# Five matrix products instead of six for each weight tile of the MLPs: high and low operand side by side in three PSUM banks

## The chip, the cores and the metric

One NeuronCore of one Trainium2 chip runs the whole program. TensorE (PE in the profile) multiplies, VectorE (DVE), ScalarE (ACT) and GpSimd (POOL) do the elementwise work, SyncE (SP) and others issue transfers. The metric is device time in microseconds (us) of one launch; lower is better.

## The reference

One inference step of two decoder layers, for a prompt of 512 tokens and 8 sample tokens, 520 columns together. What matters here is that each layer ends with the same MLP over d_model 1024 and d_ff 4096:

```python
def sq_relu_mlp(h, w_up, w_down):
    return jnp.square(jax.nn.relu(h @ w_up)) @ w_down
...
        yp = yp + rmsnorm(mp, g[1])
        ys = ys + rmsnorm(ms, g[1])
        yp = yp + rmsnorm(sq_relu_mlp(rmsnorm(yp, g[2]), w_up[layer], w_down[layer]), g[3])
        ys = ys + rmsnorm(sq_relu_mlp(rmsnorm(ys, g[2]), w_up[layer], w_down[layer]), g[3])
```

Ahead of it stand, in layer 0, attention with a paged cache and gated linear attention, and in layer 1 a recurrent block. The change touches neither.

## The kernel before

Activations lie transposed: features on the 128 partitions, the 520 columns (T) along the free side, in 8 tiles of 128 features (KT). Every product is made from two parts of each operand. A float32 value is split into a high part (type fp32r, read by TensorE at one column a step) and a low part, the rest. The product is high weight by high data, plus high weight by low data, plus low weight by high data.

Weights come in chunks of 256 output features and all 1024 inputs, 1 MB each, by SyncE's queue into RAW (two slots). ScalarE makes the high part W_hi (`split_hi`, L810), VectorE the low part W_lo (`split_lo`, L1285). A chunk has two output tiles of 128 features. For a tile, `step` (L1881) issues for each of 8 input tiles k six products of 260 columns, three pairs over the two halves of the 520 columns. They accumulate in two PSUM banks; tiles alternate between two such pairs of banks (`ch.par`), so that one is emptied while the other is filled.

An MLP is 32 chunks in 4 groups. In a group, chunks 0 to 3 are w_up: VectorE takes the relu out of PSUM, multiplies by the norm's factor and writes it to SBUF (`evicted`, L1683), ScalarE squares it (L1124), VectorE makes U_hi and U_lo of it (`raised`, L1688 and L1690). Chunks 4 to 7 are w_down: their products read U, and VectorE adds each finished tile into ACC (L1717). The first two chunks of each MLP are made by `opening`, which interleaves three tiles with the norm of the stage before.

After the last chunk of an MLP comes the norm of its output: ScalarE squares the 8 tiles of ACC (`square`, L835), TensorE sums the squares with a matrix of ones (`sum_squares`, L1865), ScalarE takes the root (L842), VectorE the inverse (L1306), TensorE spreads it over the partitions (`spread`, L1873), and VectorE scales and adds (L1310, L1316). In layer 0 ScalarE and VectorE also split half a chunk of the next stage between the sixth and the seventh square (`early_hi`, L816, and `early_lo`, L1290). In layer 1 ScalarE also writes ACCG, a scaled copy of ACC (L1237), behind each square.

Each engine's queue is an order written out by hand and runs strictly in that order. Engines wait on semaphores: `tiles_done` counts finished tiles, `banks_free` the emptied banks, `w_lo_ready` the split chunks, `sq_ready` the squares. Names that one memory region shares are aliases: RL is SQ, LL (after) is TMP.

Of the kernel before, what the change touches and what calls it, by code (L numbers as in the profile page):

```python
# [113 lines left out]
def trunk(nc, ctx, a, o):  # L114
# [29 lines left out]
    H_hi = sb("H_hi", [P, KT, T], F32R, r_h)  # L144
    H_lo = sb("H_lo", [P, KT, T], F32R, r_h + KT * TB)
# [615 lines left out]
    def _(act):  # L761
# [332 lines left out]
        def before_odd():  # L1094
# [24 lines left out]
        def mlp(layer, c0):  # L1119
            def raised(ch, i, u, count):  # L1120
                act.wait_ge(banks_free[ch.par[i]], ch.banks_free[i] + 1)
                if u >= 2:
                    act.wait_ge(u_lo_ready, count - 1)
                A(UF[:, i], RL[:, i], ACT.Square).then_inc(uf_ready, 1)  # L1124

            for g in range(4):
                for j in range(8):
                    c = c0 + 8 * g + j
                    if c > c0 and c + 1 < N_CHUNKS:
                        split_hi(Chunk(c + 1))  # L1130
                    if layer == 0 and g == 1 and j == 5:
                        before_odd()
                    if j < 4:
                        for i in range(2):
                            u = 2 * j + i
                            raised(Chunk(c), i, u, 32 * layer + 8 * g + u)
# [110 lines left out]
    def _(ve):  # L1247
# [429 lines left out]
        def mlp(layer, c0):  # L1677
# [622 lines left out]
```

## Time and profile before

| | us |
|---|---|
| median of 3 runs | 1545.1 (1544.49 to 1548.04) |
| the profiled execution, its own time | 1543.63 |
| its span, first to last instruction | 1541.8 |
| PE busy | 1406.3 (91%) |
| DVE busy | 882.3 (57%) |
| ACT busy | 516.7 (34%) |
| mean granted TensorE clock | 0.930 of full |

The span is what the trace's rows add up to; the profiled execution's own time is 1.8 us longer, and the median of the unprofiled runs 1.5 us longer again. Busy time of PE counts overlapping products once and says nothing of how near the engine is to its peak. How far apart two products start is read from how long a row of x of them lasts: start of the last minus start of the first is the row's length less one product's duration.

### The profile page before, as it was taken

The page shows a single profiled execution, that of the slowest core. Times are in us where ns is not written, and L with a number is a line of the kernel's source. Part 1 is how long each engine was busy: PE and PEld are TensorE (multiplying, and loading weights), DVE is VectorE, ACT ScalarE, POOL GpSimd, SP SyncE. Part 2 cuts the span into 40 slices and gives each one's busy share as a digit, 9 for nine tenths or more (in the row PEclk, how much of TensorE's full clock was granted, in tenths as well). Part 3 has the DMA queues.
Part 4 walks back from the last instruction along what each step waited for, and adds up shares of the span by engine and source line. Part 5 has one row for each costly group of instructions (what it writes and reads, how often), then busy time and mean ns, then how long its engine had stood idle before and what let it go on. Part 6 is the DMA issues. An engine that isn't in the chain of part 4 may idle for free.

```text
span 1541.8 us, 26106 instructions
## 1 busy us (share of the span) xinstructions
PE 1406.3 (91%) x11324; PEld 1266.3 (82%) x11324; DVE 882.3 (57%) x1156; ACT 516.7 (34%) x839; POOL 328.7 (21%) x264
## 2 busy tenths in 40 slices
PE   4999957788778698999999999899989999999997
PEld 3999933345334398999999999899989999999997
DVE  3398978766988526624435343689556344353443
ACT  3323254433423424312212122469443122131233
POOL 1085768865777100000000000000000000000000
PEclk8999979877676799999999999999999999999999
DMA  9477699988989831232322322222212323223211
GB/s 320 137 264 232 236 327 382 369 324 326 346 322 346 300 109 55 86 106 83 97 97 82 99 94 83 83 83 83 85 55 88 105 83 101 92 83 103 90 55 56
DMA packets 126856, 249.32 MB, mean 162 GB/s; under 512 B 5251, under 2 KB 107415, under 8 KB 110096
## 3 DMA queue, kind: packets, MB, share of 16 engines
q0 software_dynamic: 18432, 134.23, 22.9%
q1 hardware_dynamic: 103616, 107.13, 21.5%
q10 hardware_dynamic: 4696, 6.32, 1.3%
q8 instruction: 89, 1.46, 0.4%
q14 instruction: 23, 0.19, 0.0%
HBM read 239.99 MB, written 7.73 MB: 161 GB/s over the span
## 4 chain that ended last, share of the span: by engine, by line
PE 58%; issue 25%; DVE 7%; POOL 4%; DMA 3%; ACT 3%; ACTq 0%; POOLq 0%; DVEq 0%
PE PS L1881 46%; PE PS L2074 2%; POOL PROD L680 2%; DMA KV<-in_cache_v,CIDX 2%; DVE SC L1352 1%; PE PS L2216 1%; POOL KV L747 1%; DVE ST L1584 1%; PE PS L2061 1%; PE PS L2158 1%; DMA XSIN<-in_x_sample 1%; PE PS L1865 1%; PE PS L2179 1%; PE PS L2116 1%; PE PS L1975 1%
## 5 line engine op out<-in xcount | busy, mean ns | idle before, releaser
L1881 PE MATMUL PS<-H_hi,W_hi 128*128 128x260 f32 x1936 | 397.7, 287 | 16.7 <-DVE H_lo L1327 9.7
L1881 PE MATMUL PS<-H_hi,W_lo 128*128 128x260 f32 x1936 | 393.4, 285 | 0.0
L1881 PE MATMUL PS<-H_lo,W_hi 128*128 128x260 f32 x1936 | 393.0, 285 | 0.0
L1881 PEld LDWEIGHTS PS<-H_hi,W_hi 128*128 128x128 f32 x1936 | 303.2, 191 | 22.3 <-issue 17.7
L1881 PEld LDWEIGHTS PS<-H_hi,W_lo 128*128 128x128 f32 x1936 | 301.9, 191 | 0.0
L1881 PEld LDWEIGHTS PS<-H_lo,W_hi 128*128 128x128 f32 x1936 | 301.7, 191 | 0.0
L1285 DVE TENSOR_TENSOR W_lo<-RAW,W_hi 128x2048 fp32r<-128x2048 f32 x90 | 208.2, 2313 | 125.9 <-ACT W_hi L810 125.8
L810 ACT ACTIVATE W_hi<-RAW 128x2048 fp32r<-128x2048 f32 x90 | 171.8, 1909 | 266.1 <-PE PS L1881 265.5
L1881 PE MATMUL PS<-U_hi,W_lo 128*128 128x260 f32 x1024 | 206.4, 283 | 0.0
L1881 PE MATMUL PS<-U_lo,W_hi 128*128 128x260 f32 x1024 | 206.0, 283 | 0.0
L1881 PE MATMUL PS<-U_hi,W_hi 128*128 128x260 f32 x1024 | 206.0, 282 | 0.0
L680 POOL TENSOR_TENSOR PROD<-KV,QB 128x1024 f32<-128x1024 f32 x64 | 152.0, 2375 | 120.4 <-DVE SC L1352 91.5
L1717 DVE TENSOR_TENSOR ACC<-ACC,PS 128x520 f32<-128x520 f32 x64 | 44.6, 697 | 201.4 <-PE PS L1881 201.4
L1881 PEld LDWEIGHTS PS<-U_hi,W_hi 128*128 128x128 f32 x1024 | 157.9, 189 | 0.0
L1881 PEld LDWEIGHTS PS<-U_hi,W_lo 128*128 128x128 f32 x1024 | 157.9, 188 | 0.0
L1881 PEld LDWEIGHTS PS<-U_lo,W_hi 128*128 128x128 f32 x1024 | 157.4, 188 | 0.0
L753 POOL MEMSET ACC<- 128x4160 f32 x2 | 7.1, 3572 | 637.3 <-DVE TMP L1310 637.3
L1124 ACT ACTIVATE UF<-SQ 128x520 f32<-128x520 f32 x64 | 40.8, 639 | 253.2 <-DVE SQ L1683 253.2
L2074 PE MATMUL PS<-KV,PM 128*32 128x512 f32 x512 | 88.2, 777 | 23.4 <-DMA KV<-in_cache_v,CIDX 13.6
L1683 DVE SCALAR_TENSOR_TENSOR SQ<-PS,RS 128x520 f32<-128x520 f32 x64 | 44.6, 700 | 109.2 <-PE PS L1881 109.2
L1364 DVE TENSOR_TENSOR PROD<-KV,PS 128x1024 f32<-128x1024 f32 x64 | 77.5, 1210 | 9.0 <-ACT QB L866 8.9
L747 POOL DMA_INDIRECT KV<-in_cache_k,CIDX x64 | 70.4, 1100 | 53.8 <-DVE TMP L1310 23.1
(304 smaller groups left out, 1433.8 us busy)
## 6 DMA issues: line engine op xcount, KB each, us to landing
RAW<-in_w_up SPq DMA_DIRECT2D x32, 1024.0 KB
RAW<-in_w_down SPq DMA_DIRECT2D x32, 1024.0 KB
RAW<-in_w_in_even SPq DMA_DIRECT2D x13, 1024.0 KB
RAW<-in_w_in_odd SPq DMA_DIRECT2D x8, 1024.0 KB
RAW<-in_w_out_even SPq DMA_DIRECT2D x4, 1024.0 KB
RAW<-in_w_out_odd SPq DMA_DIRECT2D x4, 1024.0 KB
x_saved<-X ACTq DMA_DIRECT2D x1, 2080.0 KB, 9.3
X<-x_saved SPq DMA_DIRECT2D x1, 2080.0 KB, 7.8
```

The lines of the kernel that those rows point to most:

```text
L680: nc.gpsimd.tensor_tensor(PROD[:, 1], KV[i % RING][:, 2:4, :], QB[:, None, b % 2, :].to_broadcast([P, 2, 512]), ALU.mult).then_inc(prod1_r ...
L747: po.indirect_dma_start(KV[i % RING].rearrange("p n f -> p (n f)"), None, cache[kind], bass.IndirectOffsetOnAxis(ap=CIDX[:, n:n + 1], axis ...
L810: A(W_hi[:, ch.slot], RAW[:, ch.slot], ACT.Copy).then_inc(w_hi_ready, 1)
L1124: A(UF[:, i], RL[:, i], ACT.Square).then_inc(uf_ready, 1)
L1285: V.tensor_tensor(W_lo[:, ch.slot], RAW[:, ch.slot], W_hi[:, ch.slot].bitcast(F32), ALU.subtract).then_inc(w_lo_ready, 1)
L1352: V.tensor_reduce(k_scores(n, 1), PROD[:, 1].rearrange("p n (j d) -> p n j d", d=DH), AX.X, ALU.add).then_inc(prod1_used, 1)
L1364: V.tensor_tensor(PROD[:, 0], KV[i % RING][:, 0:2, :], PS[:, None, 6 + b % 2, :].to_broadcast([P, 2, 512]), ALU.mult).then_inc(k_used, 1)
L1584: V.scalar_tensor_tensor(ST[:, hp, state(tb, n + 1)], ST[:, hp, state(tb, n)], DECC[:, hp, 8 * tb + n:8 * tb + n + 1], update(n, slice(0, ...
L1683: V.scalar_tensor_tensor(pair(RL[:, i]), tile_banks(ch, i), 0.0, pair(RS[:, 1]), ALU.max, ALU.mult).then_inc(banks_free[ch.par[i]], 1)
L1717: V.tensor_tensor(pair(ACC[:, m]), pair(ACC[:, m]), banks(ch.par[i]), ALU.add).then_inc(banks_free[ch.par[i]], 1)
L1881: t = MM_(PS[:, 2 * bank + j, 0:HALF], w[:, ch.slot, k, cols], x[:, k, half], start=k == 0 and n == 0, stop=k == KT - 1 and n == 2)
L2074: t = MM_(PS[32 * pos:32 * pos + 32, 4, :], PM[:, part % 2, at:at + 32], KV[i % RING][:, pos, :], start=n % 32 == 0, stop=n % 32 == 31)
```

## The change

Chunks 2 to 31 of each MLP (the two of `opening` stay as they were) get another way of multiplying. The high and the low data lie side by side in one tensor of 1040 columns (H for H_hi and H_lo, U for U_hi and U_lo). `joint_step` sends high weight over all 1040 columns in three products (284, 284 and 472 columns) and low weight over the 520 high columns in two (284 and 236). Results of the high data stand in one bank's end and the next one's beginning, and the results of the low data behind them, through a third bank. The columns streamed stay 1560 for each k.

The two parts are added outside TensorE. ScalarE copies the part of the low data to LL (two copies, 48 and 472 columns, `low_copied`). For w_up VectorE adds the PSUM part and LL into RL and then takes relu and factor in place, in a second pass (`joint_evicted`); for w_down it adds first LL and then the PSUM part to ACC (`accumulated`). The last tile of `opening` goes to the two banks of SPREAD (`FOURTH`) and waits for their copy instead of for the first eviction. Some semaphores of other places are merged.

```diff
-    H_hi = sb("H_hi", [P, KT, T], F32R, r_h)
-    H_lo = sb("H_lo", [P, KT, T], F32R, r_h + KT * TB)
+    H = sb("H", [P, KT, 2 * T], F32R, r_h)
+    H_hi, H_lo = H[:, :, 0:T], H[:, :, T:2 * T]
...
+    CUT = 284
...
-            def raised(ch, i, u, count):
-                act.wait_ge(banks_free[ch.par[i]], ch.banks_free[i] + 1)
+            def low_copied(ch, i, q):
+                act.wait_ge(tiles_done, ch.done[i])
+                act.wait_ge(banks_free[ch.par[i]], ch.banks_free[i])
+                first, rest = joint_lo(ch.par[i])
+                A(LL[:, q % 2, 0:LO_CUT], first, ACT.Copy)
+                A(LL[:, q % 2, LO_CUT:T], rest, ACT.Copy).then_inc(ll_ready, 1)
+
+            def raised(i, u, count):
...
+                    for i in range(2):
+                        u, q = 2 * j + i, joint_tile(layer, g, j, i)
+                        if g == 0 and j < 2:
+                            act.wait_ge(banks_free[ch.par[i]], ch.banks_free[i] + 1)
+                        else:
+                            low_copied(ch, i, q)
+                            if j < 4:
+                                act.wait_ge(rl_ready, 28 * layer + 8 * g + u - 3)
+                        if j < 4:
+                            raised(i, u, 32 * layer + 8 * g + u)
...
+            def joint_evicted(ch, i, u, q, count):
+                ve.wait_ge(tiles_done, ch.done[i])
+                ve.wait_ge(ll_ready, q + 1)
+                V.tensor_tensor(RL[:, i], joint_hi(ch.par[i]), LL[:, q % 2], ALU.add).then_inc(banks_free[ch.par[i]], 1)
+                ve.wait_ge(banks_free[ch.par[i]], ch.banks_free[i] + 1)
+                V.scalar_tensor_tensor(RL[:, i], RL[:, i], 0.0, RS[:, 1], ALU.max, ALU.mult).then_inc(rl_ready, 1)
+
+            def accumulated(ch, i, m, q):
+                ve.wait_ge(ll_ready, q + 1)
+                link(V.tensor_tensor(ACC[:, m], ACC[:, m], LL[:, q % 2], ALU.add))
+                ve.wait_ge(tiles_done, ch.done[i])
+                V.tensor_tensor(ACC[:, m], ACC[:, m], joint_hi(ch.par[i]), ALU.add).then_inc(banks_free[ch.par[i]], 1)
...
-                            ve.wait_ge(tiles_done, ch.done[i])
-                            V.tensor_tensor(pair(ACC[:, m]), pair(ACC[:, m]), banks(ch.par[i]), ALU.add).then_inc(banks_free[ch.par[i]], 1)
+                            accumulated(ch, i, m, q)
...
+        def joint_step(ch, i, k, both):
+
+            cols, bank = slice(P * i, P * i + P), 3 * ch.par[i]
+            hi, lo = W_hi[:, ch.slot, k, cols], W_lo[:, ch.slot, k, cols]
+            first, last = k == 0, k == KT - 1
+            MM_(PS[:, bank, 512 - CUT:512], hi, both[:, k, 0:CUT], start=first, stop=False)
+            MM_(PS[:, bank + 1, 0:CUT], hi, both[:, k, CUT:2 * CUT], start=first, stop=False)
+            MM_(PS[:, bank + 2, 0:2 * T - 2 * CUT], hi, both[:, k, 2 * CUT:2 * T], start=first, stop=last)
+            MM_(PS[:, bank, 512 - CUT:512], lo, both[:, k, 0:CUT], start=False, stop=last)
+            t = MM_(PS[:, bank + 1, 0:T - CUT], lo, both[:, k, CUT:T], start=False, stop=last)
+            if last:
+                t.then_inc(tiles_done, 1)
...
-            pe.wait_ge(banks_free[b.par[1]], b.banks_free[1])
+            if c0 == C_IN1:
+                pe.wait_ge(banks_free[b.par[1]], b.banks_free[1])
+            else:
+                pe.wait_ge(rs_copied, opened + 1)
```

The order of instructions on TensorE for one k of a w_down tile, first before and then after (W_hi and W_lo are the weight parts, U the data):

```order
L1881 MATMUL PS<-U_hi,W_hi 128x260 x2
L1881 MATMUL PS<-U_lo,W_hi 128x260 x2
L1881 MATMUL PS<-U_hi,W_lo 128x260 x2
```

```order
L1938 MATMUL PS<-U,W_hi 128x284
L1939 MATMUL PS<-U,W_hi 128x284
L1940 MATMUL PS<-U,W_hi 128x472
L1941 MATMUL PS<-U,W_lo 128x284
L1942 MATMUL PS<-U,W_lo 128x236
```

Six products of 260 columns have become three with the high weight and two with the low weight.

The order on ScalarE at the end of layer 0's MLP, from its last weight split on. Before (L810 splits a chunk, L835 squares a tile of ACC, L816 is `early_hi`):

```order
L810 ACTIVATE W_hi<-RAW 128x2048 x4
L835 ACTIVATE SQ_START<-ACC 128x520 x6
L816 ACTIVATE W_hi<-RAW 128x8x128
L835 ACTIVATE SQ_START<-ACC 128x520 x2
L842 ACTIVATE RS<-PS,EPSC 128x130
```

After (L832, L857 and L838 are the same three; L1146 and L1147 copy the low part of a tile):

```order
L832 ACTIVATE W_hi<-RAW 128x2048
L1146 ACTIVATE TMP<-PS 128x48
L1147 ACTIVATE TMP<-PS 128x472
L1146 ACTIVATE TMP<-PS 128x48
L1147 ACTIVATE TMP<-PS 128x472
L857 ACTIVATE SQ_START<-ACC 128x520 x6
L838 ACTIVATE W_hi<-RAW 128x8x128
L857 ACTIVATE SQ_START<-ACC 128x520 x2
L864 ACTIVATE RS<-PS,EPSC 128x130
```

The squares stood behind the last split alone; now the copies of the last two tiles stand between, and each waits for its tile's products.

The order on VectorE at the same place, before (L1717 adds a tile into ACC, L1290 is `early_lo`, L1306 is the inverse of the norm) and after (L1729 and L1731 add the two parts, L1324 is `early_lo`, L1340 the inverse):

```order
L1285 TENSOR_TENSOR W_lo<-RAW,W_hi 128x2048 [waits w_hi_ready]
L1717 TENSOR_TENSOR ACC<-ACC,PS 128x520 [waits tiles_done]
L1290 TENSOR_TENSOR W_lo<-RAW,W_hi 128x8x128 [waits w_early]
L1717 TENSOR_TENSOR ACC<-ACC,PS 128x520 [waits tiles_done]
L1306 RECIPROCAL RS<-RS 128x130 [waits root_ready]
```

```order
L1319 TENSOR_TENSOR W_lo<-RAW,W_hi 128x2048 [waits w_hi_ready]
L1729 TENSOR_TENSOR ACC<-ACC,TMP 128x520 [waits ll_ready]
L1731 TENSOR_TENSOR ACC<-ACC,PS 128x520 [waits tiles_done,dve_step]
L1324 TENSOR_TENSOR W_lo<-RAW,W_hi 128x8x128 [waits w_early]
L1729 TENSOR_TENSOR ACC<-ACC,TMP 128x520 [waits ll_ready]
L1731 TENSOR_TENSOR ACC<-ACC,PS 128x520 [waits tiles_done,dve_step]
L1340 RECIPROCAL RS<-RS 128x130 [waits root_ready]
```

`early_lo` stood and stands ahead of the last tile's addition, which is now two instructions.

## Rows read from the trace of the kernel before

**Rows 1.** The page: the chain that ended last, by line.

```profile
PE PS L1881 46%; PE PS L2074 2%; POOL PROD L680 2%; DMA KV<-in_cache_v,CIDX 2%; DVE SC L1352 1%; PE PS L2216 1%; POOL KV L747 1%; DVE ST L1584 1%; PE PS L2061 1%; PE PS L2158 1%; DMA XSIN<-in_x_sample 1%; PE PS L1865 1%; PE PS L2179 1%; PE PS L2116 1%; PE PS L1975 1%
```

**Rows 2.** Window over layer 0: us, busy (x) of PE, PEld, DVE, ACT, POOL, then clock, DMA.

```profile
618.90:970.90 352.00, 351.99 (x2932) 351.86 (x2936) 151.12 (x160) 86.69 (x77) 0.00 (x0) 1.00 0.28 91
```

**Rows 3.** Chain that ended last, 612 to 971 us: start, length, what.

```profile
617.46 1.32 DVE SQ L1683 x2
...
618.91 351.99 PE PS L1881 x2928
```

**Rows 4.** Source views: duration ns min/median/max, first and last start.

```profile
L1881 PE MATMUL PS<-U_hi,W_lo x1024: 278/283/291, 648.3 to 1521.3; 128*128 128x260 f32 x171
...
L2044 PE MATMUL PS<-QES,S x64: 247/247/267, 332.6 to 363.5; 64*128 64x1 f32 x64
...
L2216 PE MATMUL PS<-UF,WG x64: 381/382/383, 1007.4 to 1061.3; 128*128 128x260 f32 x64
```

**Rows 5.** Single last products, nothing loaded behind: 1094.5 to 1094.6, then 975.48 to 975.5.

```profile
L1881 PE MATMUL PS<-H_hi,W_lo 128*128 128x260 f32 x1 | 0.3, 281 | 0.0
...
L1873 PE MATMUL PS<-RS,CONST 128*128 128x130 f32 x1 | 0.3, 275 | 0.0
```

**Rows 6.** Timelines of PE (start, length, products): how far apart they start.

```profile
1007.38 1.92 PE L2216 MATMUL PS<-UF,WG 128*128 128x260 f32 x8
...
591.79 0.83 PE L1873 MATMUL PS<-RS,CONST 128*128 128x130 f32 x6
...
343.01 1.94 PE L2044 MATMUL PS<-QES,S 64*128 64x1 f32 x16
...
979.33 0.64 PE L1881 MATMUL PS<-H_lo,W_hi 128*128 128x260 f32 x2
979.76 0.64 PE L1881 MATMUL PS<-H_hi,W_lo 128*128 128x260 f32 x2
```

**Rows 7.** Groups by line: ACT copies out of PSUM, 520 and 128 columns.

```profile
L1091 ACT ACTIVATE ACC<-PS 128x520 f32<-128x520 f32 x8 | 4.8, 604 | 51.8 <-PE PS L1881 51.8
...
L963 ACT ACTIVATE PJ<-PS,G 128x128 f32<-128x128 f32 x32 | 10.8, 363 | 26.5 <-PE PS L2089 26.4
```

**Rows 8.** Timeline of DVE behind the last w_up tile of a group.

```profile
648.01 0.70 DVE L1683 SCALAR_TENSOR_TENSOR SQ<-PS,RS 128x520 f32<-128x520 f32 x1 [3.19 <-PE PS L1881]
...
649.88 0.70 DVE L1690 TENSOR_TENSOR U_lo<-UF,U_hi 128x520 fp32r<-128x520 f32 x1
```

**Rows 9.** Timeline, end of the MLP of layer 0 (ACT and DVE rows).

```profile
961.29 3.26 ACT L835 ACTIVATE SQ_START<-ACC 128x520 f32<-128x520 f32 x6
965.23 1.06 ACT L816 ACTIVATE W_hi<-RAW 128x1024 fp32r<-128x1024 f32 x1 [0.69 <-PE PS L1881]
...
966.33 1.23 DVE L1290 TENSOR_TENSOR W_lo<-RAW,W_hi 128x1024 fp32r<-128x1024 f32 x1 [0.46 <-ACT W_hi L816]
970.94 0.70 DVE L1717 TENSOR_TENSOR ACC<-ACC,PS 128x520 f32<-128x520 f32 x1 [3.39 <-PE PS L1881]
...
972.94 0.37 ACT L842 ACTIVATE RS<-PS,EPSC 128x130 f32<-128x130 f32 x1 [0.63 <-PE PS L1865]
```

**Rows 10.** Timeline of ACT, end of the MLP of layer 1.

```profile
1500.46 0.62 ACT L835 ACTIVATE SQ_START<-ACC 128x520 f32<-128x520 f32 x1
...
1501.61 0.62 ACT L835 ACTIVATE SQ_START<-ACC 128x520 f32<-128x520 f32 x1
...
1522.38 0.64 ACT L835 ACTIVATE SQ_START<-ACC 128x520 f32<-128x520 f32 x1 [4.51 <-DVE ACC L1717]
...
1523.65 0.37 ACT L842 ACTIVATE RS<-PS,EPSC 128x130 f32<-128x130 f32 x1
```

**Rows 11.** Window with its granted clock; timeline of `spread` at either clock.

```profile
976.00:984.00 8.00, 5.25 (x26) 5.28 (x27) 7.58 (x12) 4.17 (x7) 0.00 (x0) 0.57 0.39 134
...
31.49 2.10 PE L1873 MATMUL PS<-RS,CONST 128*128 128x130 f32 x8 [2.09 <-DVE RS L1306]
...
974.37 1.16 PE L1873 MATMUL PS<-RS,CONST 128*128 128x130 f32 x8 [1.55 <-DVE RS L1306]
```

More of the change, by code:

```diff
@@ L187, in trunk @@
     RL = SQ
+    LL = TMP
     XC = UF
@@ L555, in banks, with joint_hi, joint_lo, joint_tile @@
         return PS[:, 2 * par:2 * par + 2, 0:HALF]
-    THIRD = 2
+    THIRD, FOURTH = 2, 3
     OPENINGS = (C_MLP0, C_IN1, C_MLP1)
     def tile_banks(ch, i):
-        return banks(THIRD if ch.static - 1 in OPENINGS and i == 0 else ch.par[i])
+        if ch.static - 1 in OPENINGS and i == 0:
+            return banks(THIRD)
+        return banks(FOURTH if ch.static - 1 in (C_MLP0, C_MLP1) else ch.par[i])
+    CUT = 284
+    BANKS = PS[:].rearrange("p b c -> p (b c)")
+    def joint_hi(par):
+        first = 512 * (3 * par + 1) - CUT
+        return BANKS[:, first:first + T]
+    def joint_lo(par):
+        bank = 3 * par + 1
+        return PS[:, bank, T - CUT:CUT], PS[:, bank + 1, 0:T - (2 * CUT - T)]
+    LO_CUT = 2 * CUT - T
+    def joint_tile(layer, g, j, i):
+        return 60 * layer + 16 * g + 2 * j + i - 4
     def pair(ap):
@@ L1127, in mlp @@
                 for j in range(8):
-                    c = c0 + 8 * g + j
-                    if c > c0 and c + 1 < N_CHUNKS:
-                        split_hi(Chunk(c + 1))
+                    ch = Chunk(c0 + 8 * g + j)
+                    if ch.static > c0 and ch.static + 1 < N_CHUNKS:
+                        split_hi(Chunk(ch.static + 1))
                     if layer == 0 and g == 1 and j == 5:
                         before_odd()
[L1133 to L1136, printed above, removed]
+                    for i in range(2):
[8 more added lines that the diff above has]
+                            raised(i, u, 32 * layer + 8 * g + u)
         def acc_ready(c0):
@@ L1710, in mlp @@
                         u = 2 * j + i
+                        q = joint_tile(layer, g, j, i)
                         if j < 4:
-                            evicted(ch, i)
+                            joint_evicted(ch, i, u, q, first + 8 * g + u)
                             raised(i, u, first + 8 * g + u)
@@ L1884, in step, with joint_products @@
                 t.then_inc(tiles_done, 1)
+        def joint_step(ch, i, k, both):
[9 more added lines that the diff above has]
+                t.then_inc(tiles_done, 1)
+        def joint_products(ch, both, ready=None):
+            pe.wait_ge(w_lo_ready, ch.ready)
+            for i in range(2):
+                pe.wait_ge(banks_free[ch.par[i]], ch.banks_free[i])
+                for k in range(KT):
+                    if ready and i == 0:
+                        ready(k)
+                    joint_step(ch, i, k, both)
         def products(ch, hi, lo, ready=None, after=None, together=False):
@@ L1947, in mlp @@
                 for j in range(2 if g == 0 else 0, 4):
-                    products(Chunk(c0 + j, g), H_hi, H_lo)
+                    joint_products(Chunk(c0 + 8 * g + j), H)
                 for j in range(4, 8):
-                    products(Chunk(c0 + j, g), U_hi, U_lo,
+                    joint_products(Chunk(c0 + 8 * g + j), U,
                              (lambda k, g=g: pe.wait_ge(u_lo_ready, g * 8 + (32 * layer + k + 1))) if j == 4 else None)
```

24 lines of the change are left out of this document (12 added, 12 removed).

## The prediction

> **What bounds the kernel now.** I read the page first. The products of L1881 carry 46% of the chain that ended last, more than any other line [rows 1]. The window over layer 0's MLP, from behind its opening, shows what kind of stretch that is: PE busy in all of its 352 us, at full granted clock, with VectorE at 151 and ScalarE at 87 [rows 2]. The chain says the same: 2928 products in 351.99 us with no wait between them [rows 3]. So in the dense stretches only the pace of the products counts: 351.99 / 2928 = 120.2 ns from one to the next, and 6 x 120.2 = 721 ns for one k.
>
> What makes it 120.2? At 2.4 GHz 260 columns stream in 108.3 ns, so 11.9 are added. Rows of other products split this. An f32 product takes two clock periods a column: 130 columns, again 260 periods, start (0.83 - 0.275) / 5 = 111 ns apart [rows 5, 6], only 2.7 over the streaming. Products of one single column, each with its own 128-column weight load, start (1.94 - 0.247) / 15 = 113 ns apart [rows 4, 6]; with hardly any streaming left, this is the pace of the weight loads. So 120.2 is neither the loads' pace as measured there nor streaming plus 2.7. Durations say where the other 9 ns lie: the MLP's fp32r products last 283 ns in the median [rows 4], the f32 ones of as many periods 275. And a last product, behind which no weight load starts for 0.37 us, still lasts 281, where the last f32 one lasts 275 [rows 5]. The stretch thus belongs to the fp32r stream and not to a load beside it. At half clock, 1.2 GHz, it is gone: (979.76 - 979.33) / 2 = 0.215, and 260 / 1.2 is 0.217 [rows 6].
>
> **The change part by part, on TensorE.** Per k, 1560 columns stream before and after (650 ns). Steps that change: 30 chunks x 2 tiles x 8 k x 2 layers = 960. What one product less saves depends on whether the 9.2 ns (11.9 less 2.7) come per product or per column; no fp32r product of another width than 260 stands in the trace, so I bound it.
> - All per product: 650 + 5 x 11.9 = 709.5. The 236-column one would come to 98.3 + 11.9 = 110.2, under the loads' 113, which adds 2.7: 712. Saved 9 x 960 = 8.7 us.
> - Only 2.7 per product, the rest 0.035 ns per column: 650 + 55.2 + 13.5 = 718.7, and 3.5 more for the 236-column one: 722. Lost: 0.9 us.
>
> The new widths 284 and 236 lie near 260, where both readings agree; only the 472-column product tells them apart, and no row is nearer to one end. I take the middle, 3.9 us saved.
>
> The Trainium skill, page "TensorE: Matmul & The Clock Gate", section "Back-to-back issue gap", has an isolated gap of N / 2.4 + 2.5 ns. By it a step would go from 665 to 662.5, 2.4 us in all. The trace agrees for f32 (111) and not for fp32r (120.2 where the rule has 110.8); by the rule the sum would be 1.5 us above mine.
>
> **Evictions in the middle of the MLP** cost nothing. Per tile ScalarE gets two copies. From 604 ns for 520 columns and 363 for 128 [rows 7] a column costs 0.615, so 472 columns take 0.57 and 48 take 0.31; ScalarE instructions back to back start 0.1 earlier than the one before ends (six squares in 3.26 [rows 9]), so 0.80 together. VectorE gets one pass of 0.70. The cover is the tile of 5.7 us: ScalarE's 87 of 352 us grow by 60 x 0.8 = 48, VectorE's 151 by 42. The tightest hand-over is at a group's turn, where the w_down products need U of the last w_up tile at k = 7, 7 x 0.72 - 0.3 = 4.7 us behind that tile's end. Eviction, square, cast and U_lo took 650.58 - 648.01 = 2.57 [rows 8]; with 0.80 + 0.70 and two hand-offs of 0.04 it is 4.2. It holds with half a microsecond left; without that cover each of 8 groups would pay the lateness and about 0.3 for starting again.
>
> **The end of each MLP** is where the change costs. ScalarE's queue is in strict order, and the copies for the last tile now stand ahead of all squares of ACC. They wait for the last product. Before, seven of eight squares in layer 0 were done while the last tiles were multiplied: six at 961.29, the seventh behind the split at 965.23; behind the last product, which ended at 618.91 + 351.99 = 970.90, came only 0.70 of VectorE, one square and the rest of the sum. The root started at 972.94, 2.04 later [rows 3, 9].
> - Layer 0 now, from the last product: copies 0.84; six squares, 0.53 apart, until 3.9; `early_hi` 1.06, until 5.0; `early_lo` 1.23 on VectorE, until 6.3. Only behind it in VectorE's queue come the two additions of the last tile, 1.4 with their hand-offs, until 7.7; then its square 0.68, until 8.4. The root follows 0.63 behind it, as now [rows 9]: 9.0. That is 7.0 us more. Inverse, spread, scaling and the next opening all wait for it.
> - Layer 1 now: squares and ACCG copies alternate, 1501.61 - 1500.46 = 1.15 a pair. The first starts at 0.75, the eighth at 0.75 + 7 x 1.15 = 8.8; with 0.64 and 0.63 the root comes at 10.1. Now it comes at 1523.65, the products having ended 0.77 ahead of the square at 1522.38: 2.04 [rows 10]. That is 8.1 more.
> - TensorE is idle all that time. In the idle stretch of before, the granted clock fell only at its end (mean 0.57 in 976 to 984) [rows 11]. With 7 us more it should have fallen to 1.2 GHz before `spread`, which took 1.16 at full clock and 2.10 at the half [rows 11]: 0.94 more, twice, 1.9.
>
> **Opening.** Its last tile no longer waits for the two evictions of 1.32 us at 617.46 [rows 3], but for ScalarE's copy of the norm ahead of them. Most of that wait lay behind TensorE's own work on the tile before; I take 0.3 saved in each MLP, 0.6. Bounds: nothing, and 1.4 each.
>
> **Sum** against the profiled span in the table: 1541.8 - 3.9 + 7.0 + 8.1 + 1.9 - 0.6 = 1554.3. The median of the runs stands 3.3 above that span (1545.1), so 1557.6 us.
>
> **Rivals.**
> - The products are bound by loads after all, and the change ends faster. For it: 111 and 113 lie so close together that load and stream, running side by side, could delay each other by 7 to 9 ns. Then longer products hide the loads: 3 x (118.3 + 2.7) + 199.4 + 120.2 = 683 instead of 721, saved 38.7 x 960 = 37 us, time 1545.1 + 16.4 - 37.2 = 1524. It decides once a step takes under 704 ns (16.4 us / 960). Against it: the 281 ns of a product with no load behind it, and the 113 of loads alone. The same page of the Trainium skill, section "LDWEIGHTS (loading the stationary operand)", puts 128 columns at 106.7 ns, further still from 120.2, but its section on the gap says that in a stream both operations together set the spacing. The trace has no stream that decides it. 24%.
> - The 236-column product, shorter than any fp32r product of the trace, falls to the f32 pace: (1.92 - 0.382) / 7 = 0.220 for 260 columns [rows 4, 6], 0.200 for 236, so 0.087 x 960 = 83 us more, 1641. Nothing in the rows speaks for a threshold, nothing excludes one. 5%.
> - U comes late at the groups' turns: it decides when the two copies and the added pass take 2.1 us instead of 1.6. By 0.3 us late, 8 x 0.6 = 5 us on top, 1562. 5%.
> - The ends cost less and the per-product reading holds, so that the two cancel: 1545 to 1550. It wants 8.7 saved and the ends under 13. 6%.
>
> **How the numbers follow.** My forecast has 60%. Its own range is 1550 to 1565: -8.7 to +0.9 on the products, 2.5 either way on the ends (copies, clock). With the late hand-over it makes 65%. That leaves 35% out, so the range must reach to the load-bound case and its spread: 1519 to 1565. A measurement can tell 0.3%, 4.6 us, from no change. Faster: the load-bound case, 24%. Same: most of the cancelling case and the lower tail of mine, 8%. Slower: 68%.
>
> **What would show it.** In the changed profile: the spacing in the dense stretches, at 712 to 722 ns a step if I am right and near 683 in the first rival; the duration of the 472-column product, whose median should be 283 + 88 = 371 or, stretched by column, 379. At the ends, ScalarE idle until the last product, then copies, six squares, the split, two squares, and the root 9 and 10 us behind the products; `spread` at 2.1 us. ScalarE and VectorE should otherwise keep ahead, with no wait of PE on U_lo at the groups' turns. I am wrong if longer fp32r products take only their streaming time, or if the squares start before the last product ends.

## The result and the profile after

The changed kernel takes 1561.34 us (median of 12 runs) where the kernel before takes 1546.46 (12 runs): ratio 1.0098, 95% interval 1.0078 to 1.0118. It is 14.9 us slower. I had forecast 1557.6 against a median of 1545.1, 12.5 us slower; the range, 1519 to 1565, holds it.

The page of the changed kernel; the first row answers to the span of before, the second to [rows 1].

```profile
span 1558.4 us, 24786 instructions
...
PE PS L1928 23%; PE PS L1940 7%; PE PS L1941 4%; PE PS L1938 4%; PE PS L1939 4%; PE PS L1942 3%; PE PS L2147 2%; POOL PROD L702 2%; DVE SC L1386 1%; PE PS L2231 1%; DVE ST L1618 1%; DMA KV<-in_cache_v,CIDX 1%; PE PS L2289 1%; PE PS L2134 1%; DMA XSIN<-in_x_sample 1%
```

The products of the MLPs now stand on several lines (L1938 to L1942), those of the other stages on L1928. PE's chain runs through them as before.

The window over all of layer 0's five-product steps (columns as in [rows 2]), and in it the 472-column products of U (x count, busy us, mean ns):

```profile
626.20:971.70 345.50, 345.50 (x2400) 332.05 (x2398) 184.18 (x211) 116.50 (x184) 0.00 (x0) 1.00 0.29 92
```

```profile
L1940 PE MATMUL PS<-U,W_hi 128*128 128x472 f32 x256 | 97.0, 379 | 0.0
```

TensorE is busy throughout at full clock. 2400 products are 480 steps: 345.5 / 480 = 719.8 ns, where six products took 6 x 120.14 = 720.8 (one tile of 48 every 5.7667 us). Five products a step instead of six are worth one nanosecond. The 472-column product lasts 379 ns, the value I had given for a cost by column.

ScalarE at the end of layer 0's MLP; [rows 9] has the same place of before:

```profile
971.89 0.56 ACT L1147 ACTIVATE TMP<-PS 128x472 f32<-128x472 f32 x1
972.33 3.26 ACT L857 ACTIVATE SQ_START<-ACC 128x520 f32<-128x520 f32 x6
975.49 1.05 ACT L838 ACTIVATE W_hi<-RAW 128x1024 fp32r<-128x1024 f32 x1
...
979.17 0.64 ACT L857 ACTIVATE SQ_START<-ACC 128x520 f32<-128x520 f32 x1 [2.11 <-DVE ACC L1731]
980.65 0.37 ACT L864 ACTIVATE RS<-PS,EPSC 128x130 f32<-128x130 f32 x1 [0.84 <-PE PS L1912]
```

VectorE at the same place:

```profile
976.57 1.23 DVE L1324 TENSOR_TENSOR W_lo<-RAW,W_hi 128x1024 fp32r<-128x1024 f32 x1 [8.41 <-ACT W_hi L838]
977.71 0.69 DVE L1729 TENSOR_TENSOR ACC<-ACC,TMP 128x520 f32<-128x520 f32 x1
978.44 0.70 DVE L1731 TENSOR_TENSOR ACC<-ACC,PS 128x520 f32<-128x520 f32 x1
```

Read the two together. The last product ended at 971.75. Only the low copy frees ScalarE's queue; then come six squares, `early_hi` at 975.49, `early_lo` at 976.57, and only behind that the two additions of the last tile, at 977.71 and 978.44, its square at 979.17 and the root at 980.65: 8.9 us behind the last product, not 2.04.

ScalarE at the end of layer 1's MLP ([rows 10] of before):

```profile
1529.69 0.56 ACT L1147 ACTIVATE TMP<-PS 128x472 f32<-128x472 f32 x1
1530.13 0.64 ACT L857 ACTIVATE SQ_START<-ACC 128x520 f32<-128x520 f32 x1
...
1538.15 0.64 ACT L857 ACTIVATE SQ_START<-ACC 128x520 f32<-128x520 f32 x1
...
1539.63 0.37 ACT L864 ACTIVATE RS<-PS,EPSC 128x130 f32<-128x130 f32 x1 [0.22 <-PE PS L1912]
```

Squares and ACCG copies alternate from the first to the eighth, and the root stands 1539.63 - 1529.55 = 10.08 us behind the last product.

`spread` behind the two ends ([rows 11] of before):

```profile
982.07 2.10 PE L1920 MATMUL PS<-RS,CONST 128*128 128x130 f32 x8 [1.55 <-DVE RS L1340]
...
1541.05 2.10 PE L1920 MATMUL PS<-RS,CONST 128*128 128x130 f32 x8 [1.55 <-DVE RS L1340]
```

Both take 2.10 us, the value of the half clock, where before both took 1.16; [rows 11] shows layer 0's, and this is layer 1's in the kernel before:

```profile
1525.07 1.16 PE L1873 MATMUL PS<-RS,CONST 128*128 128x130 f32 x8 [1.55 <-DVE RS L1306]
```

Put together, from the two profiled executions:

| stretch | before, us | after, us | difference |
|---|---|---|---|
| start to the end of `spread` ahead of layer 0's MLP | 616.60 | 618.24 | +1.6 |
| to the last product of that MLP | 354.30 | 353.51 | -0.8 |
| to the root | 2.04 | 8.90 | +6.9 |
| to the first product of the next opening | 5.81 | 6.75 | +0.9 |
| to the last product of layer 1's MLP | 542.86 | 542.15 | -0.7 |
| to the root | 2.04 | 10.08 | +8.0 |
| to the end | 18.15 | 18.77 | +0.6 |
| span | 1541.8 | 1558.4 | +16.6 |

The first line lies ahead of everything that the change moves, but for some merged semaphores. In the profiles of the changed kernel's fp32r forms below it varies from 610.3 to 622.3 us, so its 1.6 is no effect of the change, and the time of a single run says little within some us. Without that line the profiles differ by 15.0, and the medians by 14.9.

### The profile page after: what moved, and what is told of

Its sections match the earlier page's. It is cut to its first block, busy times and chain, and to the rows that moved or that the text cites. A ratio compares the mean times of both kernels' runs of the same rounds, so it can differ in the third digit from the quotient of the medians.

```text
span 1558.4 us, 24786 instructions
## 1 busy us (share of the span) xinstructions
PE 1408.4 (90%) x10364; PEld 1238.7 (79%) x10364; DVE 965.1 (62%) x1276; ACT 592.8 (38%) x1079; POOL 330.6 (21%) x264
## 4 chain that ended last, share of the span: by engine, by line
PE 57%; issue 26%; DVE 8%; POOL 3%; ACT 3%; DMA 2%; ACTq 0%; POOLq 0%; another core or an unknown queue 0%; DVEq 0%
PE PS L1928 23%; PE PS L1940 7%; PE PS L1941 4%; PE PS L1938 4%; PE PS L1939 4%; PE PS L1942 3%; PE PS L2147 2%; POOL PROD L702 2%; DVE SC L1386 1%; PE PS L2231 1%; DVE ST L1618 1%; DMA KV<-in_cache_v,CIDX 1%; PE PS L2289 1%; PE PS L2134 1%; DMA XSIN<-in_x_sample 1%
## 5 line engine op out<-in xcount | busy, mean ns | idle before, releaser
L1928 PE MATMUL PS<-H,W_hi 128*128 128x260 f32 x2080 | 345.6, 289 | 16.4 <-DVE H L1361 9.7
L1928 PEld LDWEIGHTS PS<-H,W_hi 128*128 128x128 f32 x2080 | 293.4, 194 | 21.7 <-issue 17.1
L1928 PE MATMUL PS<-H,W_lo 128*128 128x260 f32 x1040 | 212.9, 287 | 0.0
L1940 PE MATMUL PS<-U,W_hi 128*128 128x472 f32 x512 | 194.0, 379 | 0.0
L832 ACT ACTIVATE W_hi<-RAW 128x2048 fp32r<-128x2048 f32 x90 | 171.8, 1909 | 1.6 <-PE PS L1928 0.9
L1940 PE MATMUL PS<-H,W_hi 128*128 128x472 f32 x448 | 169.8, 379 | 0.0
L1146 ACT ACTIVATE TMP<-PS 128x48 f32<-128x48 f32 x120 | 25.2, 210 | 366.5 <-PE PS L1942 366.5
L1928 PEld LDWEIGHTS PS<-H,W_lo 128*128 128x128 f32 x1040 | 164.4, 193 | 0.0
L1729 DVE TENSOR_TENSOR ACC<-ACC,TMP 128x520 f32<-128x520 f32 x64 | 44.7, 699 | 173.1 <-ACT TMP L1147 173.1
L1941 PE MATMUL PS<-U,W_lo 128*128 128x284 f32 x512 | 150.7, 294 | 0.0
L1938 PE MATMUL PS<-U,W_hi 128*128 128x284 f32 x512 | 150.2, 293 | 0.0
L1939 PE MATMUL PS<-U,W_hi 128*128 128x284 f32 x512 | 149.7, 292 | 0.0
L1942 PE MATMUL PS<-U,W_lo 128*128 128x236 f32 x512 | 139.9, 273 | 0.0
L1938 PE MATMUL PS<-H,W_hi 128*128 128x284 f32 x448 | 131.4, 293 | 0.0
L1939 PE MATMUL PS<-H,W_hi 128*128 128x284 f32 x448 | 131.0, 292 | 0.0
L1942 PE MATMUL PS<-H,W_lo 128*128 128x236 f32 x448 | 122.4, 273 | 0.0
L2147 PE MATMUL PS<-KV,PM 128*32 128x512 f32 x512 | 88.4, 779 | 25.4 <-DMA KV<-in_cache_v,CIDX 14.9
L1942 PEld LDWEIGHTS PS<-U,W_lo 128*128 128x128 f32 x512 | 96.2, 188 | 14.1
```

What stands on the lines that cost most here:

```text
L832: A(W_hi[:, ch.slot], RAW[:, ch.slot], ACT.Copy).then_inc(w_hi_ready, 1)
L1146: A(LL[:, q % 2, 0:LO_CUT], first, ACT.Copy)
L1729: link(V.tensor_tensor(ACC[:, m], ACC[:, m], LL[:, q % 2], ALU.add))
L1928: t = MM_(PS[:, 2 * bank + j, 0:HALF], w[:, ch.slot, k, cols], x[:, k, half], start=k == 0 and n == 0, stop=k == KT - 1 and n == 2)
L1938: MM_(PS[:, bank, 512 - CUT:512], hi, both[:, k, 0:CUT], start=first, stop=False)
L1939: MM_(PS[:, bank + 1, 0:CUT], hi, both[:, k, CUT:2 * CUT], start=first, stop=False)
```

## The experiments

Where a ratio is given, it is that of several runs of a kernel to several of the kernel before, with its 95% interval; the other times are of a single run. "Step" is the time for one k in the dense stretch, worked out from VectorE's evictions in one w_down group: first to last start, by the number of tiles between and by 8.

### The order of ScalarE's queue

**squares_held**: the kernel before, six products, with one wait ahead of the squares of either MLP.

```diff
         mlp(0, C_MLP0)
+        act.wait_ge(tiles_done, first_tile(C_IN1))
         for kt in range(KT):
...
         mlp(1, C_MLP1)
+        act.wait_ge(tiles_done, first_tile(N_CHUNKS))
         for kt in range(KT):
```

> The kernel before (six products, one eviction), with one wait added: ScalarE waits for the last product of each MLP before it squares tile 0 of ACC. Theory (the order of ScalarE's queue alone costs the ends, and not the copies or the third bank): root behind the last product by 7.6 us in layer 0 (six squares 3.3, early_hi 1.0, early_lo 1.2, addition 0.7, square 0.65, sum 0.8) and by 9.5 us in layer 1 instead of 2.04, and spread 0.9 and 0.6 us longer by its clock: 14.5 us in all, ratio 1.009. Rival (the squares' wait is only part, the two-part eviction carries the rest): less than 9 us, ratio under 1.006.

Measured: ratio 1.010 (1.0076 to 1.0124). ScalarE, layer 0's end, then layer 1's root:

```profile
969.51 3.27 ACT L835 ACTIVATE SQ_START<-ACC 128x520 f32<-128x520 f32 x6 [9.55 <-PE PS L1883]
...
975.63 0.64 ACT L835 ACTIVATE SQ_START<-ACC 128x520 f32<-128x520 f32 x1 [1.37 <-DVE ACC L1719]
977.11 0.37 ACT L842 ACTIVATE RS<-PS,EPSC 128x130 f32<-128x130 f32 x1 [0.84 <-PE PS L1867]
...
1536.37 0.37 ACT L842 ACTIVATE RS<-PS,EPSC 128x130 f32<-128x130 f32 x1 [0.22 <-PE PS L1867]
```

The last products ended at 969.48 and 1526.84, so the roots stand 7.63 and 9.53 us behind them, and `spread` took 2.10 both times. The kernel before is made as slow as the changed one by its squares' order alone. The low copy and the second addition make the rest of an end: 8.90 - 7.63 = 1.3 and 10.08 - 9.53 = 0.55.

**ends_moved**: the changed kernel with the low copy of the last tile behind the squares of tiles 0 to 6.

```diff
-                        else:
+                        elif (g, j, i) != (3, 7, 1):
                             low_copied(ch, i, q)
...
         for kt in range(KT):
+            if kt == 7:
+                last_low_copied()
             acc_ready(C_IN1 - 4)(act, kt)
```

> The changed kernel, but ScalarE copies the low part of each MLP's last tile behind the squares of tiles 0 to 6 of ACC instead of ahead of them. Theory (queue order costs the ends): from the last product to the start of the root 3.6 us in both layers (copies 0.7, two additions 1.45, square 0.64, sum and hand-offs 0.8) instead of 8.9 and 10.1, and the spread back near 1.17 us instead of 2.12; together 5.3 + 6.4 + 1.5 = 13 us less than the changed kernel, 0.1% above the kernel before (ratio 1.001). Rival (the ends are long because VectorE's two passes and the third bank are slow, not because of the order): the ends stay above 6 us and under 5 us are won in all (ratio above 1.006).

Measured: ratio 1.004 (1.002 to 1.006). ScalarE at the end of layer 0, then of layer 1:

```profile
968.99 0.56 ACT L1147 ACTIVATE TMP<-PS 128x472 f32<-128x472 f32 x1
...
972.29 0.37 ACT L864 ACTIVATE RS<-PS,EPSC 128x130 f32<-128x130 f32 x1 [0.61 <-PE PS L1920]
...
1514.26 0.56 ACT L1147 ACTIVATE TMP<-PS 128x472 f32<-128x472 f32 x1
1514.71 0.64 ACT L857 ACTIVATE SQ_START<-ACC 128x520 f32<-128x520 f32 x1
...
1522.83 0.55 ACT L1147 ACTIVATE TMP<-PS 128x472 f32<-128x472 f32 x1
1524.88 0.64 ACT L857 ACTIVATE SQ_START<-ACC 128x520 f32<-128x520 f32 x1 [1.50 <-DVE ACC L1739]
...
1526.35 0.37 ACT L864 ACTIVATE RS<-PS,EPSC 128x130 f32<-128x130 f32 x1 [0.22 <-PE PS L1920]
```

Layer 0 did what was expected: the root 3.44 us behind the last product, `spread` at 1.16. Layer 1 did not: 6.47, and `spread` still 2.10, so some 10 of the 13 us expected came back (5.5 and 3.6 at the roots, 0.9 at `spread`). The low copy of tile 6 (1514.26) still stands ahead of all squares, and seven pairs of square and ACCG from 1514.71 take until 1522.8, longer than the one tile of 5.76 us left. My expectation had priced the last tile's copy only and overlooked the copy ahead of it.

**best_joint**: CUT at 264 (below), and for the last tile VectorE adds the PSUM part while ScalarE copies the second piece; ScalarE signals either piece.

```diff
-    CUT = 284
+    CUT = 264
...
+                if ch.static - c0 == 31 and i == 1:
+                    ve.wait_ge(ll_ready, q + 1 + layer)
+                    link(V.tensor_tensor(ACC[:, m], ACC[:, m], joint_hi(ch.par[i]), ALU.add))
+                    ve.wait_ge(ll_ready, q + 2 + layer)
+                    V.tensor_tensor(ACC[:, m], ACC[:, m], LL[:, q % 2], ALU.add).then_inc(banks_free[ch.par[i]], 1)
+                    return
```

> The changed kernel with the best of what the runs showed: CUT at 264 (step of 718.25 instead of 719.8), the last tile's low copy behind the squares of tiles 0 to 6, and for that tile VectorE adds the PSUM part while ScalarE copies the second piece of the low part. Theory (the products are worth 2.5 ns a step against the kernel before, 2.4 us; openings 0.5; each end costs 0.9 us more than before): 2.4 + 0.5 - 1.8 = 1 us under the kernel before, ratio 0.999, no measurable difference. Rival (there is a cost of five products in three banks that the profiles do not show): ratio over 1.003.

Measured: ratio 1.0018 (1.0003 to 1.0032); the roots 2.96 and 5.77 us behind, `spread` 1.16 and 2.10. Layer 1's end is what was missing, by 2.8 + 0.9 us.

**best_joint2**: the same, and in layer 1 each square and its ACCG copy behind the low copy of the next tile.

```diff
                         elif (g, j, i) != (3, 7, 1):
                             low_copied(ch, i, q)
+                            if layer == 1 and g == 3 and u >= 9:
+                                squared_last(u - 9)
```

> The five-product kernel with CUT at 264 and both ends mended, and in layer 1 each square and its ACCG behind the low copy of the next tile, instead of all of them behind the low copy of tile 6. Theory (that queue order is what made layer 1's end 5.8 us and kept spread at 2.1 us there): root 3.0 us behind the last product in both layers and spread at 1.16, 3.7 us less than the form with all squares behind tile 6, ratio to the kernel before 0.9990, so no measurable difference. Rival (the end of layer 1 is bound by something else): the end stays near 5.8 us and the ratio at 1.0018.

Measured: ratio 1.0005 (0.9988 to 1.0022). ScalarE at the two ends:

```profile
964.94 0.59 ACT L1155 ACTIVATE TMP<-PS 128x512 f32<-128x512 f32 x1
...
967.78 0.37 ACT L864 ACTIVATE RS<-PS,EPSC 128x130 f32<-128x130 f32 x1 [0.61 <-PE PS L1933]
...
1516.00 0.59 ACT L1155 ACTIVATE TMP<-PS 128x512 f32<-128x512 f32 x1
...
1518.85 0.37 ACT L864 ACTIVATE RS<-PS,EPSC 128x130 f32<-128x130 f32 x1
```

Both roots stand 2.96 us behind the last product (964.83 and 1515.89), as expected. `spread` in layer 0, then in layer 1:

```profile
969.21 2.10 PE L1941 MATMUL PS<-RS,CONST 128*128 128x130 f32 x8 [1.55 <-DVE RS L1355]
...
1520.27 1.16 PE L1941 MATMUL PS<-RS,CONST 128*128 128x130 f32 x8 [1.55 <-DVE RS L1355]
```

Layer 1 is back at 1.16. Layer 0 is at 2.10, although its end is as short as in best_joint, where `spread` took 1.16: the mean granted clock was 0.99 from 967.00 to 969.20 us and 0.50 from 969.20 to 971.50, so it fell just as `spread` began. A short end makes the full clock likely there and does not assure it. The best form of the change that I found is level with the kernel before, no better.

### What a product costs

**cut264** and **cut264_six**: other widths, and then one product more at the same widths. The first edit stands in both, the second in cut264_six alone.

```diff
-    CUT = 284
+    CUT = 264
...
-            MM_(PS[:, bank + 2, 0:2 * T - 2 * CUT], hi, both[:, k, 2 * CUT:2 * T], start=first, stop=last)
+            if first:
+                MM_(PS[:, bank + 2, 0:2 * T - 2 * CUT], hi, both[:, k, 2 * CUT:2 * T], start=True, stop=False)
+            else:
+                MM_(PS[:, bank + 2, 0:T - CUT], hi, both[:, k, 2 * CUT:T + CUT], start=False, stop=False)
+                MM_(PS[:, bank + 2, T - CUT:2 * T - 2 * CUT], hi, both[:, k, T + CUT:2 * T], start=False, stop=last)
```

> The changed kernel with CUT at 264: products of 264, 264, 512, 264 and 256 columns. Theory (fp32r products cost 0.4575 ns a column and 0.75 each; the 236-column one stood 3 ns above that, at the pace of the weight loads): 121.5, 121.5, 235.0, 121.5 and 117.9 ns, a step of 717.5 instead of 720.0, 2.4 us in all. Rival (the last product of a step is late for another reason than its width): the 256-column product at 121 and the step at 720.

> The same with the 512-column product in two of 256 at seven of the eight k: six products a step again. Theory (a product more costs 0.75 ns): 718.2 a step, 0.7 us in all more than the five. Rival (the prediction's lower bound, some 11 ns come with each product): 727 a step, 9 us more in all.

VectorE's additions of the PSUM part in one w_down group, for the second and the eighth tile (six tiles, 48 steps apart), in cut264 and then in cut264_six:

```profile
1403.63 0.69 DVE L1731 TENSOR_TENSOR ACC<-ACC,PS 128x520 f32<-128x520 f32 x1
...
1438.11 0.70 DVE L1731 TENSOR_TENSOR ACC<-ACC,PS 128x520 f32<-128x520 f32 x1
```

```profile
1404.69 0.70 DVE L1731 TENSOR_TENSOR ACC<-ACC,PS 128x520 f32<-128x520 f32 x1
...
1439.49 0.69 DVE L1731 TENSOR_TENSOR ACC<-ACC,PS 128x520 f32<-128x520 f32 x1
```

(1438.11 - 1403.63) / 48 = 718.3 ns, near the 717.5 of a price by column, and the 256-column product takes the 117.9 it was to take (1559.5 us for the kernel, one run). But the six-product form takes (1439.49 - 1404.69) / 48 = 725.0, and since one k in eight still has five, a six-product step is 726.0 (1561.8 us, one run). A product more costs 7.7 ns, far above the 0.75 of the expectation's theory, which falls. It lies between the prediction's two bounds for a product less or more, 2.7 and 11.9 ns, and near neither. The rival's 727 ns a step came close, its "some 11 ns" for each product did not.

**before_264** asks why six products take 720.8 in the kernel before and 726.0 here. `uneven` is true for the chunks that the changed kernel multiplies in its new way. The kernel leaves out four of the 520 columns there and shifts others; only its pace counts.

```diff
-                for j, half in enumerate(halves):
-                    t = MM_(PS[:, 2 * bank + j, 0:HALF], w[:, ch.slot, k, cols], x[:, k, half],
+                for j, half in enumerate((slice(0, 264), slice(264, T)) if uneven(ch) else halves):
+                    t = MM_(PS[:, 2 * bank + j, 0:half.stop - half.start], w[:, ch.slot, k, cols], x[:, k, half],
```

> The kernel before (six products a step, two banks), but in chunks 2 to 31 of the MLPs the two halves are 264 and 256 columns instead of 260 and 260 (the eviction still reads 260 of each, so a few columns are lost: four of the 520 are left out and others shifted). If uneven widths cost time by themselves: 726 ns a step as in the six-product form of CUT 264, 5 us more than before in all. If the cost there came of the third bank and the side-by-side data: 720.8 as before.

```profile
1399.85 0.69 DVE L1718 TENSOR_TENSOR ACC<-ACC,PS 128x520 f32<-128x520 f32 x1 [1.46 <-PE PS L1885]
...
1428.68 0.70 DVE L1718 TENSOR_TENSOR ACC<-ACC,PS 128x520 f32<-128x520 f32 x1 [5.07 <-PE PS L1885]
```

(1428.68 - 1399.85) / 40 = 720.8, unchanged (1542.2 us, one run). Halves of 264 and 256 columns cost nothing more than equal ones. The 5.2 ns belong to the new arrangement: data side by side, results across three banks, another order of banks. Which of these it is was not tried. The added copies and additions of the other engines are not the cause: in cut264_six, those six-product steps of layer 0 during which ScalarE and VectorE both stood idle take 725.4 ns too (91 steps, by the starts of their products), and in the kernel before such steps take 719.8.

**cut284_six**: the 472-column product of the changed kernel as two of 236, by the same edit.

> The changed kernel with its 472-column product in two of 236 at seven of the eight k: 284, 284, 236, 236, 284, 236. If a product more costs what it did at CUT 264 (7.7 ns a step with one such step in eight without it): 719.8 + 7 to 8 = 727. If each product under some 240 columns is also held at the loads' pace of 112 to 113 ns, three of them add 3 x 2.6: 728 to 733.

Measured: 727.3 ns (from the evictions at 1406.56 and 1441.47), so 728.4 for a six-product step, 8.6 more than five. This agrees with the 7.7 at the other widths. The rival of a loads' pace of 112 to 113 ns for each short product is not seen: the 236-column products start their followers after 109.3 to 111.7 ns in the mean over layer 0.

**cut340**: a 180-column product in each step (CUT = 340, nothing else).

> The changed kernel with CUT at 340: products of 340, 340, 360, 340 and 180 columns, 1560 in all as ever. If the weight load paces each product by itself, the one of 180 columns takes 112 ns instead of 83 and the step 719 + 28 = 747 ns, 26 us more. If loads run ahead during the longer products, or time goes by columns alone: 718 to 720.

PE over one step (start, length, line):

```profile
1430.75 0.25 PE L1942 MATMUL PS<-U,W_lo 128*128 128x180 f32 x1
1430.83 0.35 PE L1938 MATMUL PS<-U,W_hi 128*128 128x340 f32 x1
1431.01 0.32 PE L1939 MATMUL PS<-U,W_hi 128*128 128x340 f32 x1
1431.17 0.33 PE L1940 MATMUL PS<-U,W_hi 128*128 128x360 f32 x1
```

The step takes 741.7 ns (1584.7 us, one run), 22 more than at 284 for the same columns. The 180-column product itself does not wait: the next one starts 82 ns behind it. The one after that is late: 184 ns (1430.83 to 1431.01) where 340-column products else start some 155 apart. The time of a short product is thus owed and paid one product later, as if the weights of that one were not loaded yet. No run tests that reading. The first expectation holds roughly in the sum (22 ns more where it had 28) and not in the place.

**bf16**: all parts in bfloat16, less exact, in the changed arrangement; the `bitcast(F32)` of the high parts, by which VectorE read them as float32, falls away.

```diff
-F32R = mybir.dt.float32r
+F32R = mybir.dt.bfloat16
```

> The changed kernel with every high and low part kept as bfloat16 instead of fp32r: the same products, columns and loads, of 2-byte numbers, with less exact sums. Theory (what a product takes beyond its columns / 2.4 GHz, some 12 ns, comes of 4-byte operands): a step at 650 + 5 x 2.7 = 664 ns, up to 680 if the 236-column product is held by its load, 40 to 55 us less in all where the evictions still keep up. Rival (it comes with each product or load, whatever the type): the step stays at 715 to 720.

```profile
1430.88 0.36 PE L1940 MATMUL PS<-U,W_hi 128*128 128x472 bf16 x1
1431.07 0.28 PE L1941 MATMUL PS<-U,W_lo 128*128 128x284 bf16 x1
1431.19 0.27 PE L1942 MATMUL PS<-U,W_lo 128*128 128x236 bf16 x1
1431.30 0.28 PE L1938 MATMUL PS<-U,W_hi 128*128 128x284 bf16 x1
```

The step falls to 666.5 ns, and the kernel to 1485.1 us in its one run, 76 less than the changed kernel. The 960 steps make 51 us of these, within the 40 to 55 expected; the edit changes the products of the other stages too. In the means over layer 0, 284-column products start 120.0 ns apart where 118.3 stream (123.7 ahead of the 472-column one), 472 columns 198.3 where 196.7 stream; 236 columns take 104.4 for 98.3. By the Trainium skill, page "TensorE: Matmul & The Clock Gate", section "Back-to-back issue gap", a product of N columns by itself starts its follower after N / 2.4 + 2.5 ns: the 120.0 and the 198.3 agree within a nanosecond, the 123.7 and the 104.4 lie 3 to 4 above, and the fp32r rows (131.0, 216.7) 10 and 17.5 above. So the surplus over bfloat16, 10.7 ns a product in the mean, comes of 4-byte operands. Whether of their loads or of their stream is open: this run changed both.

### What was hidden

**opening_only**: the kernel before with the opening's last tile in SPREAD's banks.

```diff
-            pe.wait_ge(banks_free[b.par[1]], b.banks_free[1])
+            if c0 == C_IN1:
+                pe.wait_ge(banks_free[b.par[1]], b.banks_free[1])
+            else:
+                pe.wait_ge(rs_copied, opened + 1)
...
-                step(b, 1, b.par[1], k, H_hi, H_lo)
+                step(b, 1, b.par[1] if c0 == C_IN1 else FOURTH, k, H_hi, H_lo)
```

> The kernel before, with nothing changed but the last tile of the two MLP openings, which goes to the banks of SPREAD and waits for their copy instead of for the first eviction. Theory (the wait of 1.58 us between the spread's products and the last tile was all on the path): 1.6 us saved in each MLP, 3.2 in all, ratio 0.998. Rival (as the prediction had it, most of that wait is hidden and 0.3 is saved in each): 0.6 us, ratio 0.9996. The trace tells them apart: TensorE idle or not between the spread and the last tile, and no idle moved to the tile behind.

Measured: ratio 0.9988 (0.9966 to 1.001). The interval holds both expected ratios, so the trace has to decide. In it the stretch from `spread` to the last product fell from 354.30 to 353.87 us in layer 0 and from 354.31 to 353.87 in layer 1, 0.4 each. The theory in this expectation had misread [rows 3]: from 617.33 to 618.77 TensorE was multiplying two other tiles, which the chain, following VectorE there, doesn't list. The prediction's 0.3 for each opening was the better reading.

**evict_more**: VectorE's first pass three times.

```diff
+    EXTRA = 2
...
+                for _ in range(EXTRA):
+                    link(V.tensor_tensor(RL[:, i], joint_hi(ch.par[i]), LL[:, q % 2], ALU.add))
                 V.tensor_tensor(RL[:, i], joint_hi(ch.par[i]), LL[:, q % 2], ALU.add).then_inc(banks_free[ch.par[i]], 1)
```

> The changed kernel with VectorE's first pass over each w_up tile (PSUM part plus LL) done three times: 1.46 us more for each tile. In the changed kernel U_lo of the last w_up tile is ready 0.76 us ahead of the products that need it. Theory (the evictions are hidden with that slack and no more): TensorE waits 0.7 us at each of 8 groups' turns, 6 us in all, and nowhere else. Rival (the added pass already costs something elsewhere, or there is more cover): no wait at the turns, or waits at other tiles too, 10 us and more.

The slack in the changed kernel, VectorE's U_lo and then the eighth step of the tile that reads it:

```profile
652.60 0.70 DVE L1737 TENSOR_TENSOR U<-UF,U 128x520 fp32r<-128x520 f32 x1
...
654.06 0.30 PE L1938 MATMUL PS<-U,W_hi 128*128 128x284 f32 x1
```

0.70 from 652.60 is 653.30, and 654.06 is 0.76 later. With the two more passes the kernel took 1583.59 us; TensorE's waits over layer 0, and VectorE's weight splits one chunk apart:

```profile
PE PS L1941 <- DVE U L1740: 7.3, 4, 2.0
...
644.03 2.29 DVE L1320 TENSOR_TENSOR W_lo<-RAW,W_hi 128x2048 fp32r<-128x2048 f32 x1 [0.64 <-ACT W_hi L833]
...
656.32 2.29 DVE L1320 TENSOR_TENSOR W_lo<-RAW,W_hi 128x2048 fp32r<-128x2048 f32 x1 [0.64 <-ACT W_hi L833]
```

In the changed kernel, for comparison:

```profile
642.42 2.29 DVE L1319 TENSOR_TENSOR W_lo<-RAW,W_hi 128x2048 fp32r<-128x2048 f32 x1 [0.64 <-ACT W_hi L832]
...
649.99 0.70 DVE L1723 TENSOR_TENSOR SQ<-PS,TMP 128x520 f32<-128x520 f32 x1 [2.06 <-ACT TMP L1147]
...
653.94 2.29 DVE L1319 TENSOR_TENSOR W_lo<-RAW,W_hi 128x2048 fp32r<-128x2048 f32 x1 [0.64 <-ACT W_hi L832]
```

The span grew by 23.4 us, 2.9 for each group, not 0.7: the rival's "10 us and more" is what came. The four longest waits of layer 0 stand at the groups' turns, and three of 0.5 us one tile ahead of a turn, but VectorE had fallen behind all through the w_up chunks: 656.32 - 644.03 = 12.29 us from split to split, where TensorE needs 11.52 for two tiles (653.94 - 642.42). VectorE had 2.06 us of idle in a chunk that was no short hand-over (ahead of 649.99), and 2.92 were added: 0.86 too much, where 0.77 a chunk is measured. Of the 10.9 us by which layer 0's stretch grew, the row above puts 7.3 down to U_lo, and the three waits ahead of the turns are 1.5; the rest is not traced. The true cover is 1.0 us a tile, for the chunk as a whole; the 0.76 at the turn is a second limit, met later. The pass that the change itself adds is hidden: its profile has no wait of TensorE in the dense stretch.

## Why the prediction came out as it did

The direction, the place and nearly the size were right: 12.5 forecast, 14.9 measured.

- **Ends of the MLPs.** Forecast +7.0 and +8.1, measured +6.9 and +8.0. The root was to stand 9.0 and 10.1 us behind the last product; it stands 8.90 and 10.08. squares_held shows the cause, the queue's order.
- **The clock at `spread`.** Forecast 0.94 twice. 2.10 instead of 1.16 us in both layers. Over all profiles here `spread` took 2.10 behind each of the 18 MLP ends of 5.77 us and more, and 1.16 behind nine of the ten ends of 2.04 to 3.44 us; the tenth is layer 0 of best_joint2. The 0.94 thus followed from the long ends, as forecast, though a short end is no warrant against it.
- **The products.** This is the term that was mis-sized. Forecast "3.9 us saved", between 8.7 saved and 0.9 lost. Measured 1.0 ns a step, 1.0 us. Both bounds supposed that a product's time hangs on its own width and kind alone, and the middle between them, chosen for want of a row, was 2.9 us off. Within one arrangement the sixth product costs 7.7 and 8.6 ns, between the 2.7 of the one bound and the 11.9 of the other. The new arrangement gives most of it back: 5.2 ns at CUT 264 and 728.4 - 720.8 = 7.6 at CUT 284. Nothing of the trace of before could show that, since it has fp32r products of the MLP's kind in one arrangement only. The 379 ns of the 472-column product, taken alone, looked like a price by column and misled me in the expectations of cut264_six.
- **Opening.** Forecast 0.6 in both. The two stretches gave 0.8 and 0.7, of which the products are 0.5 each: 0.5 is left.
- **Evictions at nothing.** No wait of TensorE stands in the dense stretches. The half microsecond that I gave the hand-over was 0.76.
- **The rivals.** Load-bound products (1524): the step was to be 683 ns, and is 719.8; cut340 has a late product only behind a short one. Nor is the 113 ns between single-column products a floor for each product: there a follower starts after 82. The 236-column product at the f32 pace (1641): it starts its follower after 111.8 ns, not 200. U late at the turns (1562): the time came near it, 1561.3, by luck; the mechanism did not happen. Cancelling (1545 to 1550): it wanted 8.7 us saved and ends under 13, and had 1.0 and 14.9.

The sum by terms: -1.0 products, +6.9, +8.0, +1.5 with the slower `spread` (0.9 and 0.6 net), -0.5 opening: 14.9.

## What to carry to other kernels

Before a step is put into a strict queue, list what stands behind it: here a copy that costs nothing in the middle of a stage cost 7 and 8 us at the ends, because seven ready squares stood behind it. And judge a cover by the busiest engine's whole period as well as by the next deadline. When the instruction count falls but the streamed columns stay, measure a short run of the new arrangement first: one product fewer saved 8 ns a step, and the new places took 5 to 8 back.

## What the runs showed of the hardware

- fp32r products in a dense stream take 5.6 to 18.4 ns more each than bfloat16 ones of the same widths and arrangement: the step of 1560 columns takes 719.8 ns against 666.5, at the same full granted clock.
- Six fp32r products over 1560 columns take 720.8 ns in two alternating banks (before_264) and 726.0 with the data side by side and three banks (cut264_six), at the same widths of 264 and 256. The cause within that arrangement stays open.
- A 180-column product does not hold its follower (82 ns), but the one behind it (184 instead of 155 ns).
- The granted clock does not fall at a fixed distance behind the last dense product: with the same end of 2.96 us in layer 0, `spread` ran before its fall in best_joint (1.16 us) and behind it in best_joint2 (2.10 us).
